# Expert stage on one core: 88 places, up tiles in a loop on TensorE, turning and scattering moved

## The reference

```python
def moe_swiglu(h, w_router, w_gate, w_up, w_down):
    logits = (h @ w_router).astype(jnp.float32)
    top_val, top_idx = lax.top_k(logits, TOP_K)
    top_w = jax.nn.softmax(top_val, axis=-1)
    gates = jnp.sum(jax.nn.one_hot(top_idx, N_EXPERTS) * top_w[..., None], axis=-2)
    out = jnp.zeros_like(h)
    for e in range(N_EXPERTS):
        y = (silu(h @ w_gate[e]) * (h @ w_up[e])) @ w_down[e]
        out = out + gates[..., e:e + 1] * y
    return out
```

## Time and profile before

| what | us |
|---|---|
| median of 3 runs | 3143.01 |
| lowest, highest | 3138.71, 3143.89 |
| the profiled execution | 3139.56 |
| its span, first to last instruction | 3137.6 |
| mean granted TensorE clock | 0.960 |
| expert stage, up and down tiles, in the profile | 665.7 to 1653.2 |

### The profile page before, as it was taken

The page is one execution under the profiler, slowest core; times in us unless marked ns, Lnnn a source line. Parts: engine busy times, 40 slices in busy tenths (PEclk is TensorE's granted clock), DMA queues, the critical chain, the costliest instruction groups (busy, mean ns, idle before and its releaser), DMA issues. The chain is left out here.

```text
span 3137.6 us, 70498 instructions
## 1 busy us (share of the span) xinstructions
PE 2915.2 (93%) x31472; PEld 2178.4 (69%) x31472; DVE 624.6 (20%) x1701; ACT 396.7 (13%) x1066; POOL 32.7 (1%) x46
## 2 busy tenths in 40 slices
PE   5889999999999999999999996887999999889999
PEld 2567856679989899999996465774544444545883
DVE  0121001121100000001001135663222210223331
ACT  1110001110000000000001123332111100122210
POOL 0000000000000000000000000000000000000000
PEclk9899999999999999999999987888999999999999
DMA  8783434259989899999992110000112202311442
GB/s 346 303 333 134 149 146 147 106 213 347 365 339 369 337 369 351 365 364 358 357 385 91 67 41 15 2 2 25 70 67 81 81 27 81 134 67 54 144 151 80
DMA packets 80495, 585.60 MB, mean 187 GB/s; under 512 B 8912, under 2 KB 8912, under 8 KB 10064
## 3 DMA queue, kind: packets, MB, share of 16 engines
q1 hardware_dynamic: 79920, 580.15, 48.6%
q10 hardware_dynamic: 288, 1.05, 0.1%
HBM read 580.11 MB, written 1.05 MB: 185 GB/s over the span
## 5 line engine op out<-in xcount | busy, mean ns | idle before, releaser
L1448 PE MATMUL ps<-arena,ring 128*64 128x96 f32 x14336 | 601.9, 246 | 9.3 <-issue 8.1
L1448 PEld LDWEIGHTS ps<-arena,ring 128*64 128x64 f32 x14336 | 594.5, 137 | 20.3 <-issue 18.5
L2500 PE MATMUL ps<-hT,ring 128*128 128x256 f32 (+2 forms) x1472 | 455.3, 472 | 5.6 <-ACT hT L464 3.4
L2500 PEld LDWEIGHTS ps<-hT,ring 128*128 128x128 f32 x1472 | 274.5, 190 | 185.2 <-issue 166.3
L352 PE MATMUL ps<-ring,arena 128*128 128x512 f32 x896 | 388.3, 594 | 4.4 <-DVE small L996 4.4
L352 PEld LDWEIGHTS ps<-ring,arena 128*128 128x128 f32 x896 | 170.4, 191 | 216.4 <-issue 214.9
L1482 PE MATMUL ps<-arena,ring 128*64 128x96 f32 x7168 | 302.7, 246 | 10.2 <-issue 9.3
L1482 PEld LDWEIGHTS ps<-arena,ring 128*64 128x64 f32 x7168 | 297.8, 137 | 14.4 <-issue 13.4
L198 PE MATMUL ps<-hT,ring 128*128 128x256 f32 (+1 forms) x608 | 192.9, 478 | 8.2 <-ACT arena L749 4.0
L198 PEld LDWEIGHTS ps<-hT,ring 128*128 128x128 f32 x608 | 117.2, 194 | 81.8 <-issue 72.3
L1520 DVE TENSOR_TENSOR arena<-arena,ps 128x96 f32<-128x96 f32 x224 | 57.0, 255 | 574.2 <-ACT arena L1498 574.2
(11 more groups left out here) (508 smaller groups left out, 2267.9 us busy)
## 6 DMA issues: line engine op xcount, KB each, us to landing
ring<-in_stream SPq DMA_DIRECT2D x547, 1024.0 KB, 6.0
par<-in_params SPq DMA_DIRECT2D x1, 3397.0 KB, 28.7
h<-in_x ACTq DMA_DIRECT2D x2, 512.0 KB, 7.8
cx<-in_ctx SPq DMA_DIRECT2D x2, 512.0 KB, 29.5
out<-h SPq DMA_DIRECT2D x4, 256.0 KB, 2.0
par<-in_params SPq DMA_DIRECT2D x1, 941.0 KB, 6.0
```

The lines of the kernel that those rows point to most:

```text
L1448: last = nc.tensor.matmul(ps[m:m + 64, 4 + s % 2, half * P:half * P + CAP], w[:, k, half * P + m:half * P + m + 64], hTe[:, k, :], start=( ...
L2500: last = nc.tensor.matmul(ps[:, 2 * BANKS_CONV[f % RING] + half, tok], w[:, k, half * P:half * P + P], hT[:, k, tok], start=(k == 0), stop ...
```

## The change

`CAP` becomes 88. The up tiles of experts 1 to 7 become a loop on TensorE of four turns, each with the code of seven tiles, one for each slot of the ring; expert 0 stays written out. Waits in the loop compare semaphores with values made from the turn's register, and `moe_hid` becomes seven semaphores, one for each place in a turn. The seven tiles of a turn use banks 4, 5, 4, 5, 4, 5, 6. As nothing can stand between tiles of one turn only, turning and scattering of expert e - 1 move behind the up tiles of expert e: turn of half 1 (bank 7), gather of the next expert, turn of half 0 (bank 6), scattering of halves 1 and 0, then the down tiles. The gather now waits for the `hid` of tile 26 and not of tile 27. In expert 0 the second `place_products` goes from behind tile 14 to behind tile 15, and tiles 13, 20 and 27, which use bank 6, wait for what VectorE and ScalarE take from banks 6 and 7.

```diff
 EPS = 1e-6
-CAP = 96
+CAP = 88
 GH = 4
...
         moe_silu = sem("moe_silu")
-        moe_hid = sem("moe_hid")
+        moe_hid = [sem(f"moe_hid{j}") for j in range(RING)]
         moe_sums = sem("moe_sums")
...
         wait_of = lambda k: 16 * ((moe_t0 + k) // RING + 1)
+        assert nf % RING == 0 and per % RING == 0
+        turns = nf // RING
+        up_bank = (4, 5, 4, 5, 4, 5, 6)
+        def hid_made(eng, m):
+            if m >= 0:
+                eng.wait_ge(moe_hid[m % RING], m // RING + 1)
...
-        TURN_AT, SPREAD_AT = 1, 5
         GATES_AT, PICKS_AT = 0, 2
-        ROWS_AT = (10, 14)
+        ROWS_AT = (10, 15)
         CTX_AT = (18, 22)
...
-        def turn(pe, e):
-            for q in range(2):
-                pe.wait_ge(moe_sums, 2 * e + q + 1)
-                for k in range(4 * q, 4 * q + 4):
-                    last = nc.tensor.transpose(ps[0:CAP, 6 + q, (k % 4) * P:(k % 4) * P + P], yT[:, k, :], ident)
-                last.then_inc(moe_turned, 1)
-        def spread_rows(pe, e):
+        def turn(pe, e, nth, q):
+            pe.wait_ge(moe_sums, 2 * e + 2 if nth else 2 * e + q + 1)
+            for k in range(4 * q, 4 * q + 4):
+                last = nc.tensor.transpose(ps[0:CAP, 6 + q, (k % 4) * P:(k % 4) * P + P], yT[:, k, :], ident)
+            last.then_inc(moe_turned, 1)
+        def spread_rows(pe, e, halves):
             marks = []
-            for half in range(2):
-                pe.wait_ge(moe_y, 2 * e + half + 1)
+            for nth, half in enumerate(halves):
+                pe.wait_ge(moe_y, 2 * e + nth + 1)
                 for t in range(TT):
...
                                             skip_group_check=True)
-                    if e == EXPERTS - 1 and half == 1:
+                    if e == EXPERTS - 1 and nth == 1:
                         marks.append(pe_done.by(last))
...
-        def copy_turned(dve, e):
-            for q in range(2):
-                dve.wait_ge(moe_turned, 2 * e + q + 1)
-                nc.vector.tensor_copy(y[0:CAP, q * 512:q * 512 + 512], ps[0:CAP, 6 + q, :]).then_inc(moe_y, 1)
+        def copy_turned(dve, e, nth, q):
+            dve.wait_ge(moe_turned, 2 * e + nth + 1)
+            nc.vector.tensor_copy(y[0:CAP, q * 512:q * 512 + 512], ps[0:CAP, 6 + q, :]).then_inc(moe_y, 1)
+        def up_products(w, j):
+            for half in range(2):
+                for k in range(KT):
+                    for m in (0, 64):
+                        last = nc.tensor.matmul(ps[m:m + 64, up_bank[j], half * P:half * P + CAP],
+                                                w[:, k, half * P + m:half * P + m + 64], hTe[:, k, :],
+                                                start=(k == 0), stop=(k == KT - 1), skip_group_check=True)
+            last.then_inc(tile_used.sem, 1)
...
                 pe.wait_ge(moe_tokens, e + 1)
-                for s in range(nf):
+                for s in range(nf if e == 0 else 0):
                     pe.wait_ge(landed[slot(at + s)], wait_of(at + s))
-                    w = ring[:, slot(at + s), :].rearrange("p (k n) -> p k n", k=KT)
-                    pe.wait_ge(moe_hid, e * nf + s + 1)
-                    for half in range(2):
-                        for k in range(KT):
-                            for m in (0, 64):
-                                last = nc.tensor.matmul(ps[m:m + 64, 4 + s % 2, half * P:half * P + CAP],
-                                                        w[:, k, half * P + m:half * P + m + 64], hTe[:, k, :],
-                                                        start=(k == 0), stop=(k == KT - 1), skip_group_check=True)
-                    last.then_inc(tile_used.sem, 1)
-                    if e and s == TURN_AT:
-                        turn(pe, e - 1)
-                    if e and s == SPREAD_AT:
-                        spread_rows(pe, e - 1)
-                    if e == 0 and s in ROWS_AT:
+                    hid_made(pe, s - (2 if 2 <= s % RING < 6 else RING if s % RING == 6 else 3))
+                    if up_bank[s % RING] == 6 and s >= RING:
+                        pe.wait_ge(moe_rows_out, 2 * sum(at_ < s for at_ in ROWS_AT))
+                        pe.wait_ge(moe_ctx_out, 2 * sum(at_ < s for at_ in CTX_AT))
+                    up_products(ring[:, slot(at + s), :].rearrange("p (k n) -> p k n", k=KT), s % RING)
+                    if s in ROWS_AT + CTX_AT:
+                        hid_made(pe, max(m for m in range(RING - 1, s, RING)))
+                    if s in ROWS_AT:
                         n = ROWS_AT.index(s)
...
                         place_products(4 * n).then_inc(moe_rows, 1)
-                    if e == 0 and s in CTX_AT:
+                    if s in CTX_AT:
                         n = CTX_AT.index(s)
...
                         ctx_products(n).then_inc(moe_ctx, 1)
-                    if e == 1 and s == 0:
-                        read_flag(pe, "pe")
-                pe.wait_ge(moe_hid, e * nf + (nf + 2))
+                if e:
+                    with pe.Fori(turns * e, turns * e + turns) as g:
+                        for j in range(RING):
+                            pe.wait_ge(landed[slot(j)], g * 16 + (32 * e + wait_of(j)))
+                            if 2 <= j < 6:
+                                pe.wait_ge(moe_hid[j - 2], g + 1)
+                            else:
+                                pe.wait_ge(moe_hid[6 if j == 6 else j + 4], g)
+                            if j == 6:
+                                pe.wait_ge(moe_sums, 2 * e)
+                            up_products(ring[:, slot(j), :].rearrange("p (k n) -> p k n", k=KT), j)
+                if e == 1:
+                    read_flag(pe, "pe")
+                if e:
+                    turn(pe, e - 1, 0, 1)
+                hid_made(pe, e * nf + nf - 2)
                 if e + 1 < EXPERTS:
                     gather(pe, e + 1)
+                hid_made(pe, e * nf + nf - 1)
+                if e:
+                    turn(pe, e - 1, 1, 0)
+                    spread_rows(pe, e - 1, (1, 0))
...
                         last.then_inc(tile_used.sem, 1)
-            turn(pe, EXPERTS - 1)
-            last_spread.extend(spread_rows(pe, EXPERTS - 1))
+            for q in range(2):
+                turn(pe, EXPERTS - 1, 0, q)
+            last_spread.extend(spread_rows(pe, EXPERTS - 1, (0, 1)))
...
-                    act.wait_ge(moe_hid, e * nf + s + 1)
-                    nc.scalar.activation(sg[:, s % 2, :], ps[:, 4 + s % 2, 0:CAP], ACT.Silu).then_inc(moe_silu, 1)
+                    hid_made(act, e * nf + s - 2)
+                    nc.scalar.activation(sg[:, s % 2, :], ps[:, up_bank[s % RING], 0:CAP], ACT.Silu).then_inc(moe_silu, 1)
                     if e == 0 and s - 1 in ROWS_AT:
...
             wait_marks(dve, routed)
-            dve.sem_inc(moe_hid, 2)
             dve.wait_ge(moe_gathered, 1)
...
                     nc.vector.tensor_tensor(hid[:, s, :], sg[:, s % 2, :],
-                                            ps[:, 4 + s % 2, P:P + CAP], ALU.mult).then_inc(moe_hid, 1)
-                    if e and s == TURN_AT:
-                        copy_turned(dve, e - 1)
+                                            ps[:, up_bank[s % RING], P:P + CAP], ALU.mult).then_inc(moe_hid[s % RING], 1)
                     if e == 0 and s == GATES_AT:
...
                         read_flag(dve, "dve")
+                if e:
+                    copy_turned(dve, e - 1, 0, 1)
                 if e + 1 < EXPERTS:
...
                 if e:
+                    copy_turned(dve, e - 1, 1, 0)
                     dve.wait_ge(moe_spread, e)
...
                         .then_inc(moe_sums, 1)
-            copy_turned(dve, EXPERTS - 1)
+            for q in range(2):
+                copy_turned(dve, EXPERTS - 1, q, q)
             dve.wait_ge(moe_ctx_out, 4)
```

## The result

| what | before | after |
|---|---|---|
| median, us (4 runs each) | 3140.86 | 3090.76 |
| lowest, highest | 3136.42, 3143.89 | 3087.43, 3093.76 |
| ratio, 95% interval | | 0.9841 [0.9822, 0.9861] |
| span of the profiled execution | 3137.6 | 3091.6 |
| first up to last down product | 987.5 | 934.7 |

The change saves 50 us. The time lies in the range of 3045 to 3212, but the forecast was 3170, slower than before, and the kernel got faster. The profiled execution is the slowest of its four, 3.0 us above the median.

A forecast was written before the change was run, and what follows sets the result against it. TensorE, busy 93% of the span, was taken as the bound. Terms -75.4 - 5.2 + 2.5 + 63 + 15 + 27 = +26.9 on the profiled 3139.6 gave 3166.5, 3170 as median; range 3045 to 3212.

The forecast's parts named there:

- 88 columns, gather with it: Expert stage and gather: each record's step falls by 3.42 us per thousand-fold ns count, 75.4 us saved, lower end 55.
- turning and scattering: Between the tiles: record times follow 128 and 512 columns, not 88, and their waits are covered, so 0.
- gather's wait: Before the gather: it now waits for the tile before, 2.4 us older, which saves 5.2 us.
- tile 20 of expert 0: Up tiles of expert 0: the tile waits until the banks of `ctx_products` are empty, plus 2.5 us, once.
- jumps back: Loop of up tiles: 21 backward jumps fetch code again at 3.0 us each, plus 63 us.
- rest of a page behind a jump: After each jump: half the time the landing page's rest is shorter than the next page's wait, plus 15 us.
- clock behind the jumps: After jumps: TensorE's pause lowers the granted clock at half of 21 jumps, 2.6 us each, plus 27 us.
- other page gaps: Remaining tiles: shorter tiles show late pages more, pauses give transfers air; set at 0, ends -12 and +20.
- The turn stays in the store: Rival for the loop: jumps under 0.2 us, no clock loss, most pages not brought again; 3055 us, chance 0.27.
- resident rival: The rival "The turn stays in the store": about 12 us of page gaps also saved, 3055 us, chance 0.27.
- Pages are brought again, but cheaply: Rival for the loop: 1.5 us a jump, too short to lower the clock; 3097 us, chance 0.15.
- The transfers' bound: Rival in the expert stage: tiles ask 435 GB/s, best seen 396, so weights and pages bind; 3254 us, chance 0.05.

The follow-up runs named there:

- e_body14: Kernel after with two turns of 14 up tiles instead of four of seven, one jump back per expert: 3193.58 us, ratio 1.0186.
- b_loop96: Kernel after with CAP back at 96, so the loop alone: 3118.46 us, ratio 0.9939.
- a_before88: Kernel before with only CAP = 88, no loop, nothing moved: 3136.50 us, ratio 1.000.
- k_moved88: Kernel before with 88 places, turning moved behind up tile 26 and scattering behind 27, all written out: 3160.50 us, ratio 1.0056.
- d_half_weights: Kernel after, with only the first half of each weight tile transferred from the expert stage's seventh tile on: 3030.96 us, one run.
- j_after_again: Kernel after run once more, unchanged, on the chip of three other runs: 3088.44 us, ratio 0.9826.
- c_straight88: Kernel after with its loop written out, same order, banks, waits and 88 places: 3171.92 us, ratio 1.0097.

## Why the prediction was wrong, point by point

| term | forecast, us | measured |
|---|---|---|
| 88 columns, gather with it | -75.4 | -72.5 (products 70.7, gather 1.8) |
| turning and scattering | 0 | -2.6 (+1.4, -4.0) |
| gather's wait | -5.2 | -4.6 |
| tile 20 of expert 0 | +2.5 | +2.2 |
| jumps back | +63 | 0 |
| rest of a page behind a jump | +15 | 0 |
| clock behind the jumps | +27 | 0 |
| other page gaps | 0 (-12 to +20) | +24.8 |
| sum | +26.9 | -52.8 in the stage, -46.0 in the span |

**The columns: right.** 37.69 ns a step for 37.6 forecast, and 72.5 us for 75.4; the weight load does not hold it, the router's products had bounded it well.

**The small waits: right.** The gathering's line has no idle time in the stage. Both copies of the turned result are covered, and the wait at tile 20 is 2.2 us.

**The failed step** is the price of a jump: "I take 3.0 us, nearer the far branch than nothing, since in the sequence of the earlier trace rows the page needed is always the one just being brought: no sign of a deep store." With its 15 and 27 us that is 105 of the 3170, and the runs show none of it: no gap at a jump, 74 pages fewer, the clock at 1.00 through the whole stage. In straight code the next page is always a new one, so its lateness tells how far ahead pages are fetched and nothing of how many are kept. The earlier trace rows was a branch to code that had never been there. Neither row could show the store, and I read the absence as evidence. The rival "The turn stays in the store" was right in its mechanism, with q8's fall of 74 packets where it said some 75, and wrong by 36 us in its time. The forecast's own test, 21 gaps of under 45 us or falling packets, names it as wrong. e_body14 shows that such jumps exist, at 3.3 us net for 5.0, where the turn isn't kept.

Two near hits are luck. The measured 3090.8 lies in the range only because the range reached down to the resident rival. And it is nearest to the 3097 of "Pages are brought again, but cheaply", whose mechanism did not take place: no page of a turn was brought again.

In the Trainium skill, "Runtime: NRT & Kernel Launch", Instruction fetch mechanics, says that a taken branch outside the current two-page window forces a fetch. The 53.15 us with three jumps over 3.7 pages and one packet contradict that for TensorE; e_body14's turn of 7.3 pages behaves as it says.

**The second miss** is a term that I set at 0 with +20 as its end, and that made the resident rival's 3055 too fast by 36 us. It counted 12 us of gaps saved, and at 96 places b_loop96 shows 9.0. But at 88 places each page that is still brought costs 0.47 us of idle time instead of 0.14 in the stage of before. The shorter page alone, 5.07 us of work instead of 5.50, gives 0.48 in a_before88, at the same 358 GB/s as before; the move, which gave up the work between the tiles, makes it 0.62 in k_moved88. Put as pages times idle per page: before 0.14 x 173, 88 columns 0.48 x 173, moved 0.62 x 173, looped 0.47 x 99. The loop's 74 pages fewer are what turns the columns into time.

**The transfers' bound: not reached.** The transfers ran at 413 GB/s over 45 us, above the 396 that I took as the best, but with a DMA share of 1.01. TensorE used tiles at an estimated 435 GB/s there (1194 records, 64 to a tile of 1.0486 MB, in 45 us), and what lay in the ring covered the difference. TensorE did not wait for a weight tile in the stage after, and SyncE still waited 475.1 us for up tiles to be used (541.4 before). What I had as a rival, weights and pages in each other's way, exists at the size of d_half_weights' difference, about 41 us of idle time, without weights ever being late.

**The part outside the stage** varies between profiles from 2141.6 to 2160.2 us, and is 6.9 us longer after than before. No place of the code is needed for that: j_after_again is the same kernel and has 2150.9, where before has 2150.0. The granted clock goes with it. Outside the stage it was at its lower level for 246.5 us before, 261.7 after and 236.8 in j_after_again; over the fourteen profiles, from 217.4 us (e_body14, the shortest rest) to 268.6 (c_straight88), the rest grows by about 0.35 us for each such microsecond, with a correlation of 0.91. Why the clock was lower for longer in some executions is open.

**Still open.** Why a page costs 0.62 us idle where it is brought in 173 pieces and 0.47 in 99 was not separated: the loop leaves the fetches in clusters of four and five with 50 us of rest.

## What to carry to other kernels

Straight code on the engine that sets the end is a stream of its own, and it competes with the weights: before making the work between two page edges shorter, count q8's packets and the "issue" idle per page, since what a faster step gains can be lost there in full (a_before88). A loop whose turn the engine keeps takes its repeated pages out of the sum, and one that is too long is worse than straight code (e_body14), so measure the packets of the looped kernel first. Absence of a sign in straight code says nothing on what a jump back costs.

## What the runs showed of the hardware

- TensorE runs a turn of 3.7 pages of 16.4 KB again without fetching it, and jumps back in it without a gap; a turn of some 7.3 pages is fetched in full every time, with 4.7 to 6.1 us idle at the jump in six of its seven experts, and the granted clock at its lower level behind each of the six.
- With 64 weight columns a record takes 41.05 ns at 96 moving columns and 37.69 ns at 88.
- The fetch of a page is delayed by other transfers: 99 pages cost 46.2 us idle beside 377 GB/s and 5.5 beside 201 GB/s; 173 pages 104.5 beside 349 and 174 pages 18.2 beside 198.
- At most two 1 MB tiles under way gave 361 GB/s and starved TensorE by 31 us; three gave 381 and starved it by nothing.
